# Attention with keys and queries kept once as high and low parts, logits and values in three passes

## The reference

```python
h = rmsnorm(x, norm_g)
xa, ga, q, ckv, gb, qi, ki, wi = split(h @ w_in)
# group A: causal convolution of 4 taps, two block-diagonal gates, real-gated linear recurrence
ya = rglru(xa) * silu(ga)
# group B: an indexer scores every causal key, each query keeps 256 keys of the shared latent c
c = rmsnorm(ckv)                                  # [1024, 256]
sel = top_k(sum_h relu(qi . ki) * wi, 256)
logits = (q @ w_uk) . c[sel] * 128**-0.5 + rel_bias[bucket(distance)]
o = softmax(logits) @ c[sel]                      # per head, [1024, 256]
yb = (o @ w_uv) * silu(gb)
x = x + concat(ya, yb) @ w_out
return rmsnorm(x, final_norm_g)
```

## Time and profile before

| | |
|---|---|
| median of the runs | 1614.35 us (1614.35, 1612.88, 1614.55) |
| the profiled execution | 1613.75 us; its span 1612.1 us, mean granted TensorE clock 0.995 |
| TensorE (PE), matmuls | 1580.3 us busy, 98% of the span, 7488 instructions |
| TensorE weight loads (PEld) | 1319.5 us, 82% |
| VectorE (DVE) | 847.6 us, 53% |
| GpSimd (POOL) | 645.1 us, 40% |
| ScalarE (ACT) | 581.5 us, 36% |
| chain that ended last | PE 90%, issue 4%, VectorE 2%, ScalarE 2%, GpSimd 1%, DMA 1% |

### The profile page before, as it was taken

One profiled execution on the slowest core, in us unless ns is written; L12 is line 12 of the kernel. 1 busy time (PEld: TensorE's weight loads), 2 busy tenths in 40 slices (PEclk: granted clock), 3 DMA queues, 4 the chain that ended last, 5 costly groups with the idle time before them and its releaser, 6 DMA issues.

```text
span 1612.1 us, 21577 instructions
## 1 busy us (share of the span) xinstructions
PE 1580.3 (98%) x7488; PEld 1319.5 (82%) x7488; DVE 847.6 (53%) x1483; ACT 581.5 (36%) x846; POOL 645.1 (40%) x477
## 2 busy tenths in 40 slices
PE   7999999999999999999999999999999899999998
PEld 6788999888888888888888888777776788888886
DVE  5347555577777877875555554377678000040003
ACT  6344555443444443332111111355555122222321
POOL 4334444434445444533444434212123244444650
PEclk9999999999999999999999999999999999999999
DMA  7212111122212122223222221322222522337322
GB/s 260 73 46 72 46 39 39 33 56 63 62 56 62 36 65 68 68 85 98 72 78 72 73 76 59 111 66 82 68 79 92 219 94 95 102 112 293 129 81 104
DMA packets 132345, 140.37 MB, mean 87 GB/s; under 512 B 8534, under 2 KB 103880, under 8 KB 130248
## 3 DMA queue, kind: packets, MB, share of 16 engines
q1 hardware_dynamic: 130760, 135.51, 26.4%
q0 software_dynamic: 1536, 4.20, 0.8%
HBM read 115.04 MB, written 24.64 MB: 87 GB/s over the span
## 4 chain that ended last, share of the span: by engine, by line
PE 90%; issue 4%; DVE 2%; ACT 2%; POOL 1%; DMA 1%; SPq 0%; DVEq 0%; ACTq 0%; POOLq 0%
PE ps L1099 17%; PE ps L1101 17%; PE ps L1100 17%; PE ps L1329 6%; PE ps L1330 6%; PE ps L1331 6%; PE ps L1294 4%; PE ps L1317 3%; PE ps L1203 2%; PE ps L1205 2%; PE ps L1281 2%; PE ps L1301 1%; PE ps L1421 1%; PE ps L1419 1%; PE ps L1420 1%
## 5 line engine op out<-in xcount | busy, mean ns | idle before, releaser
L1099 PE MATMUL ps<-hT_hi,w_lo 128*128 128x512 f32 (+1 forms) x1344 | 511.3, 380 | 0.0
L1100 PE MATMUL ps<-hT_lo,w_hi 128*128 128x512 f32 (+1 forms) x1344 | 509.2, 379 | 0.0
L1101 PE MATMUL ps<-hT_hi,w_hi 128*128 128x512 f32 (+1 forms) x1344 | 509.2, 379 | 0.0
L695 POOL TENSOR_TENSOR w_lo<-w_raw,w_hi 128x512 fp32r<-128x512 f32 x168 | 237.0, 1411 | 554.7 <-ACT w_hi L792 554.7
L1099 PEld LDWEIGHTS ps<-hT_hi,w_lo 128*128 128x128 f32 x1344 | 252.3, 188 | 44.7 <-issue 1.6
L1100 PEld LDWEIGHTS ps<-hT_lo,w_hi 128*128 128x128 f32 x1344 | 252.4, 188 | 43.4 <-issue 0.2
L1101 PEld LDWEIGHTS ps<-hT_hi,w_hi 128*128 128x128 f32 x1344 | 252.3, 188 | 42.5
L792 ACT ACTIVATE w_hi<-w_raw 128x512 fp32r<-128x512 f32 x168 | 105.9, 631 | 483.2 <-PE ps L1101 353.6
L693 POOL TENSOR_TENSOR w_raw<-w_raw,g_col 128x512 f32<-128x512 f32 x168 | 200.0, 1191 | 7.6 <-DMA w_raw<-in_w_in 7.6
L1329 PE MATMUL ps<-wo_hi,hT_lo 128*128 128x512 f32 x448 | 175.8, 392 | 4.2 <-POOL wo_lo L724 4.1
L1719 DVE TENSOR_TENSOR res<-ps,res 128x512 f32<-128x512 f32 x32 | 21.9, 691 | 294.9 <-PE ps L1331 244.8
(11 more groups left out here) (196 smaller groups left out, 1814.0 us busy)
## 6 DMA issues: line engine op xcount, KB each, us to landing
w_raw<-in_w_in SPq DMA_DIRECT2D x168, 256.0 KB, 2.8
wo_raw<-in_w_out SPq DMA_DIRECT2D x64, 512.0 KB, 3.6
xin<-in_x SPq DMA_DIRECT2D x8, 1024.0 KB, 6.9
res<-in_x SPq DMA_DIRECT2D x8, 1024.0 KB, 9.5
out<-res SPq DMA_DIRECT2D x16, 512.0 KB, 3.9
y_lru_dram<-sg SPq DMA_DIRECT2D x8, 512.0 KB, 2.8
q_dram<-av SPq DMA_DIRECT2D x8, 512.0 KB, 3.7
gate_dram<-rg SPq DMA_DIRECT2D x8, 512.0 KB, 4.2
```

Source lines behind the costliest of these rows:

```text
L695: nc.gpsimd.tensor_tensor(w_lo[:, j, :, :], part, w_hi[:, j, :, :].bitcast(F32), ALU.subtract).then_inc(w_lo_s, 1)
L1099: nc.tensor.matmul(o, wlo, hi, start=(kt == 0), stop=False)
L1100: nc.tensor.matmul(o, whi, lo, start=False, stop=False)
L1101: return nc.tensor.matmul(o, whi, hi, start=False, stop=(kt == KT - 1))
```

## The change

- **Logits** are three fp32r passes. Keys are kept as k_hi and k_lo (high_k on ScalarE, low_k on VectorE), queries as q_hi and q_lo, cut in the projection turns (ScalarE writes q_out_hi, VectorE q_out_lo in low_q) and stored as two tensors. There is one copy of k_hi, k_lo, q_hi, q_lo where kT and qT were double.
- **Values** are made for two heads at once (PAIRS = 4), in three fp32r passes of 256 columns, from hT_hi, hT_lo and wv_hi, wv_lo. In heads 0 to 5 the slots after blocks 0 and 1 each hold one quarter of the next pair's values. ScalarE copies each to vP, of which there are two.
- **Keys** of the next head move from the slot after block 0 into the slot after turn_p(h, 5), in two halves (keys_half), each into the half of X[1] where read_out(h, 0) and read_out(h, 1) stood.
- **Weights**: the parts of w_uk and w_uv are made once, beside attention projection turns 0 and 1, and stored to DRAM; wk_hi, wk_lo, wv_hi, wv_lo are loaded per head or pair. high_wk and low_wk go away.
- **Recurrent outputs**: high_y on ScalarE and low_y on GpSimd cut y in the recurrent stage, from the buffer sg, and both parts are stored. In the heads they are only loaded, into hT_hi and hT_lo.
- **Output stage**: EARLY has two groups in place of three; buffers lie elsewhere; the loads of w_out wait for other things.
- The loops over pairs of heads are written out for the eight heads.

The core of the diff (removed lines of pe_head and act_head are left out; the listing has them):

```diff
-EARLY = [(0, 0), (0, 1), (1, 0)]
+EARLY = [(0, 0), (0, 1)]
...
-        kT = [s3(f"kT{i}", [P, S]) for i in range(2)]
-        vN = [s3(f"vN{i}", [P, QB, HD]) for i in range(2)]
+        vP1 = s3("vP1", [P, QB, 2, HD])
+        k_hi = s3("k_hi", [P, S], F32R)
+        k_lo = s3("k_lo", [P, S], F32R)
+        vP0 = s3("vP0", [P, QB, 2, HD])
+        vP = [vP0, vP1]
...
-        qT = [qT0, qT1]
...
+        q_hi = s3("q_hi", [P, S], F32R)
+        q_lo = s3("q_lo", [P, S], F32R)
...
             with sp.Fori(1, G) as g:
                 lru_loads(g)
-                sp.wait_ge(y_lru, g + 1)
-                sp.dma_start(yl_d[ds(g - 1, 1)].rearrange("o p s -> (o p) s"), sg[:, :]).then_inc(y_st, 16)
                 gate_loads(g)
+                y_stores(g - 1)
...
+            def q_stores(h):
                 sp.wait_ge(pj_free[1], h + T_ATT // 2 + 2)
-                sp.dma_start(q_d[ds(h, 1)].rearrange("o p s -> (o p) s"), av[:, :]).then_inc(q_st, 16)
+                sp.dma_start(qh_d[ds(h, 1)].rearrange("o p s -> (o p) s"), q_out_hi[:, :].bitcast(F32)).then_inc(q_hi_st, 16)
+                sp.dma_start(ql_d[ds(h, 1)].rearrange("o p s -> (o p) s"), q_out_lo[:, :].bitcast(F32)).then_inc(q_lo_st, 16)
...
             att_loads(0)
-            sp.wait_ge(y_lru, G + 1)
-            sp.dma_start(yl_d[G - 1], sg[:, :]).then_inc(y_st, 16)
-
             sp.dma_start(wuk[:, :, :], a["w_uk"][0].rearrange("h d c -> d h c")).then_inc(wuk_in, 16)
+            y_stores(G - 1)
...
+            def head_loads(h):
+
+                sp.wait_ge(k_mm_s, 2 * h + 2)
+                wk_loads(h + 1)
+                sp.wait_ge(lg_mm, 8 * h + 4)
+                q_loads(h + 1, 0)
+                if h > 0:
+                    sp.wait_ge(lg_used, 8 * h)
+                tb_load(h + 1)
+                if h == 0:
+                    sp.wait_ge(v_mm_s, 4)
+                    wv_loads(1)
+                if h < G - CT:
+                    y_loads(h, y_ld)
+                if h in (1, 3):
+                    sp.wait_ge(v_mm_s, 2 * h + 6)
+                    wv_loads((h + 3) // 2)
+                sp.wait_ge(lg_mm, 8 * h + 8)
+                q_loads(h + 1, 1)
+
+            for h in range(NH - 1):
+                head_loads(h)
...
+            def low_y(g):
+
+                pool.wait_ge(y_hi_s, g + 1)
+                nc.gpsimd.tensor_tensor(y_lo[:, :], sg[:, :], y_hi[:, :].bitcast(F32), ALU.subtract).then_inc(y_lo_s, 1)
+
+            with pool.Fori(1, T_LRU + 2) as t:
+                low(t)
+            with pool.Fori(1, G) as g:
+                low(g * 2 + T_LRU)
+                low(g * 2 + (T_LRU + 1))
+                low_y(g - 1)
+            low(T_ATT)
+            low_y(G - 1)
...
+            def high_y(g):
+                act.wait_ge(y_lru, g + 2)
+                nc.scalar.activation(y_hi[:, :], sg[:, :], ACT.Copy).then_inc(y_hi_s, 1)
+
             def lru(g, first=False):
                 par = lambda k: lru_p[:, k, ds(g, 1)]
                 if not first:
-                    high(g * 2 + (T_LRU + 1))
+                    high(g * 2 + (T_LRU + 1), range(2))
+                    high_y(g - 1)
+                    high(g * 2 + (T_LRU + 1), range(2, PIECES))
...
+            def high_k(h, k):
+
+                act.wait_ge(k_mm_s, 2 * h + k + 1)
+                part = slice(k * NT, (k + 1) * NT)
+                nc.scalar.activation(k_hi[:, part], X[1][:, part], ACT.Copy).then_inc(k_hi_s, 1)
+
+            def copy_v(i, n, bank):
+
+                act.wait_ge(v_mm_s, 4 * i + n + 1)
+                nc.scalar.activation(vP[i % 2][:, 2 * n:2 * n + 2, :, :].rearrange("p t o d -> p (t o d)"), bank,
+                                     ACT.Copy).then_inc(v_cp, 1)
...
+            def act_head(h):
+                last = h == NH - 1
                 for q in range(QB):
                     p_copy(h, q)
                     if q + 1 == QB and not last:
                         softexp(h + 1, 0)
                         softexp(h + 1, 1)
...
+                    elif q + 2 < QB and q not in (2, 5):
                         softexp(h, q + 2)
...
+                    if q < 2 and h < NH - 2:
+                        copy_v(h // 2 + 1, 2 * (h % 2) + q, X[1][:, q * NT:(q + 1) * NT])
                     if q == 1:
+                        softexp(h, 4)
+                    if last and q == 3:
+                        act.wait_ge(ro_mm, 4 * (NH - 2) + 4)
+                        out_high(0, [0])
+                    if q == 5:
                         if not last:
...
+                            high_k(h + 1, 0)
+                        softexp(h, 7)
                         if not last:
...
+                            high_k(h + 1, 1)
+                        else:
+                            out_high(0, [1])
...
+            def keys_half(h, k):
+
+                pe.wait_ge(wk_ld, 32 * h + 32)
+                if h > 0:
+                    pe.wait_ge(o_used, 4 * h + 1 + k)
+                keys(X[1][:, k * NT:(k + 1) * NT], k).then_inc(k_mm_s, 1)
+
+            def values(i, n, bank):
+
+
+                pe.wait_ge(wv_ld, 32 * i + 32)
+                for s in range(2):
+                    tok = slice((2 * n + s) * P, (2 * n + s + 1) * P)
+                    o = bank[:, s * 2 * HD:(s + 1) * 2 * HD]
+                    for t in range(CT):
+                        hi, lo = (hT[:, G - CT + t, tok] for hT in (hT_hi, hT_lo))
+                        whi, wlo = (w[:, t, :, :].rearrange("p o d -> p (o d)") for w in (wv_hi, wv_lo))
+                        nc.tensor.matmul(o, lo, whi, start=(t == 0), stop=False)
+                        nc.tensor.matmul(o, hi, wlo, start=False, stop=False)
+                        last = nc.tensor.matmul(o, hi, whi, start=False, stop=(t == CT - 1))
+                last.then_inc(v_mm_s, 1)
+
+            def logits(h, q):
                 w = (q + 1) * P
-                if q == 0:
-                    pe.wait_ge(qb_ld[p], turn * 32 + 32)
-                    pe.wait_ge(kv_cp, 4 * h + 2)
+                if q % 4 == 0:
+                    pe.wait_ge(q_ld[q // 4], 32 * h + 32)
+                    pe.wait_ge(k_lo_s, 2 * h + q // 4 + 1)
                 pe.wait_ge(p_cp, 8 * h + q + 5 - LAST[q])
+                tok = slice(q * P, (q + 1) * P)
                 for n in range(0, w, NT):
                     e = min(n + NT, w)
-                    last = nc.tensor.matmul(LG[q][:, n:e], qT[p][:, q * P:(q + 1) * P], kT[p][:, n:e],
-                                            start=True, stop=True)
+                    nc.tensor.matmul(LG[q][:, n:e], q_lo[:, tok], k_hi[:, n:e], start=True, stop=False)
+                    nc.tensor.matmul(LG[q][:, n:e], q_hi[:, tok], k_lo[:, n:e], start=False, stop=False)
+                    last = nc.tensor.matmul(LG[q][:, n:e], q_hi[:, tok], k_hi[:, n:e], start=False, stop=True)
                 last.then_inc(lg_mm, 1)
...
                 pe.wait_ge(p_cp, 8 * h + 2 * pr + 6)
                 if pr == 0:
-                    pe.wait_ge(kv_cp, 4 * h + 4)
-                if pr < 2 and not last_head:
-                    pe.wait_ge(kv_cp, 4 * h + pr + 7)
+                    pe.wait_ge(v_cp, 4 * (h // 2) + 4)
+                if pr < 2 and h < NH - 2:
+                    pe.wait_ge(v_cp, 2 * h + pr + 5)
+                elif pr >= 2 and h < NH - 1:
+                    pe.wait_ge(k_lo_s, 2 * h + pr + 1)
                 else:
                     pe.wait_ge(o_used, 4 * h + pr + 3)
...
+            def pe_head(h):
+                last = h == NH - 1
                 for q in range(QB):
                     if q > 0:
                         turn_p(h, q)
                     if q in (3, 4, 6):
...
+                        read_out(h, {3: 0, 4: 1, 6: 2}[q])
                     if 0 < q < QB - AHEAD:
...
+                        logits(h, q + AHEAD)
+                    elif q > 5 and not last:
+                        logits(h + 1, 2 * q - 12)
+                        logits(h + 1, 2 * q - 11)
+                    if q < 2 and h < NH - 2:
+                        if h > 0:
+                            pe.wait_ge(o_used, 4 * h + q + 3)
+                        else:
+                            pe.wait_ge(v_cp, q + 3)
+                        values(h // 2 + 1, 2 * (h % 2) + q, X[1][:, q * NT:(q + 1) * NT])
+                    if q == 5 and not last:
+                        keys_half(h + 1, 0)
+                        keys_half(h + 1, 1)
+                    if last and q > 5:
+                        out_early(0, q - 6)
+                read_out(h, 3)
                 if not last:
                     turn_p(h + 1, 0)
...
+            keys_half(0, 0)
+            keys_half(0, 1)
+            for n in range(2):
+                values(0, n, X[0][:, n * NT:(n + 1) * NT])
             pe.wait_ge(pj_free[0], TILES // 2 + 2)
             pe.wait_ge(pj_free[1], TILES // 2 + 1)
...
+            for q in range(4):
+                logits(0, q)
+            for n in range(2):
```

(42 more changed lines are left out.)

443 lines of the change are left out of this document (210 added, 233 removed).

## The result

The changed kernel takes 1648.91 us (median of 4 runs, 1648.67 to 1650.6) against 1614.45 (4 runs, 1612.88 to 1614.94): a ratio of 1.0225, 95% interval 1.0213 to 1.0237. It is slower by 34 to 38 us where 22 were forecast. The profiled execution took 1648.99 us, its span 1647.2.

What follows compares the result with a forecast made beforehand. TensorE, busy 98%, bounded the kernel; after the change a head loop through VectorE's products and the keys would. Terms +18.2 + 2.6 + 2.5 + 2.3 - 1.0 - 2.5 = +22.1 on 1613.75 gave 1636 us, range 1620 to 1650.

Steps and rivals of the forecast that it cites:

- Keys inside the loop of the products: Heads: keys' halves wait for gated(h, 0) and gated(h, 1), TensorE waiting about 1.6 and 1.9 us; loop 29.2 us.
- The ping-pong: Heads: VectorE alternating with ScalarE, from gated(h, 3) to the end of gated(h+1, 0), takes 14.8 us.
- 29.2 instead of 26.6, 2.6 more in each of the 7 heads: Heads that make keys for a successor: serial steps lengthen the loop, +18.2 us in all, bounds +14 to +26.
- rival 2: Heads: the clock falls as well behind the two TensorE waits, 2.3 us more per head, 1652 us; chance 0.08.
- Recurrent boundary: Last recurrent turn: high_y and low_y delay the next tile's weights, TensorE waits; +2.6 us, bounds 1.3 to 3.6.
- the forecast of 0: Recurrent turns 0 to 6: high_y, low_y and the stores cost nothing because weights are far ahead; 0 us.
- Start of attention: Before and in head 0: late logits and value matmuls +2.5 us, late weights of pair 1 +2.3 us.
- The wait for the weights of pair 1: Head 0: weights load only when pair 0 is multiplied, TensorE waits 3.4 us; +2.3, bounds 1 to 4.
- Head 7: Last head: no keys there, shorter logits and no low_y on GpSimd; -1.0 us, bounds 0 to -2.
- Output: Output stage: wait for the fifth weight piece shrinks by about 1.7, clock may not fall; -2.5 us, bounds 0 to -4.
- each of eleven steps: Head loop's upper bound: 0.1 us more at each step makes 3.7 more a head, +26 us.
- Rival 1: Heads: TensorE's own work still decides and the ping-pong shrinks, -14 us, 1600 us; chance 0.13.

Runs made afterwards that it cites:

- e_fill: Changed kernel with eight unused matmuls of 512 columns on TensorE between the two halves of the keys; 1644.01 us.
- e_thin: Changed kernel with one pass instead of three in the logits of blocks 4 to 7, for timing only; 1649.73 us.
- e_swap: Changed kernel with the product gated(h, 1) ahead of the subtraction low_k(h + 1, 0) on VectorE; 1637.75 us.
- e_lowy: Changed kernel with the cut of the last recurrent output moved behind the next tile's weights on ScalarE and GpSimd; 1647.84 us.
- e_gates: Changed kernel with gated(h, 0) and gated(h, 1), each with its cut, one turn earlier in all heads but the last; 1622.30 us.
- e_best: Changed kernel with both boundaries mended and earlier products, key copies and block 2 copy; 1605.76 us, ratio 0.9954 to the kernel before.
- e_late_keys: Kernel before with only its keys moved to the slot of the change, ScalarE's copies moving along; 1625.74 us against 1612.12.

## Why the prediction was wrong in size, and right in mechanism

- **Keys inside the loop of the products: right.** Both waits, their releaser and their lengths came as forecast, and where the clock stays up the loop is 29.10 (e_fill, and 29.09 in e_thin). The ping-pong from one product to the end of the next, forecast 14.8, goes from 1142.44 to 1156.94 in the changed kernel, 14.50: ScalarE's removed copies and GpSimd's removed subtractions gave at most 0.3 there. What the forecast did not see is VectorE's own work between the two products, which takes as long as half 0 with ScalarE's copy: with the subtraction out of the way the loop is still 28.47 (e_swap).
- **The step that failed: a wait was priced at its length.** "29.2 instead of 26.6, 2.6 more in each of the 7 heads" left out that the clock falls behind it. I had this as rival 2 with a chance of 0.08 at 2.3 us a head, because the trace showed a single wait of 1.93 with no harm. It came in six of the seven heads, at 1.6, which covers the 8.9 us by which the heads exceed the forecast: from half 1 to read-out 2 it takes 3.61 us in head 3 (1160.54 to 1164.15) and 2.21 in head 0, where the clock held (1070.00, below, to the read-out at 1072.21); and read-out 2 takes 2.77 instead of 2.54.

```profile
1066.56 0.47 PE L1340 MATMUL ps<-hT_hi,wk_lo 128*128 128x512 f32 x1 [1.41 <-DVE yf L1770]
...
1070.00 0.47 PE L1340 MATMUL ps<-hT_hi,wk_lo 128*128 128x512 f32 x1 [1.83 <-DVE yf L1770]
...
1071.45 0.93 PE L1384 MATMUL ps<-ident,prob_sb 128*128 128x128 f32 x7
```

- **Recurrent boundary: wait right (2.57, forecast 2.6), term mis-sized**, 4.4, by the half clock behind it again. In the other turns the forecast of 0 held: without the wait the stretch is as long as before (e_lowy), and the convolution's taps on VectorE took 1.28 us beside low_y, as they did before.
- **Start of attention: mechanism right, sizes off.** The wait for the weights of pair 1 was 4.87, not 3.4: the second of the two loads landed 4.4 us after its issue, beside loads of queries and y, not 2.8; then the granted clock was 0.57 from 1048 to 1056 us. The term was +10.4 with the first loop, not +7.4. The logits started 6.69 us after the first key matmul, 6.29 before: +0.4 for +0.9.
- **Head 7: right (-1.1). Output: -0.7 for -2.5, by a cost that the forecast did not have.** The wait for the fifth piece of w_out went from 4.09 to 2.60 and no low clock follows it, as forecast, yet the 1440 matmuls from there to the end of the span took 337.8 us instead of 336.8. They are slower one by one, at full clock and without a wait: a hundred w_out matmuls take 22.92 us from start to start in the changed kernel and 22.67 before, which is 3.1 us over the 1248 of them. e_fill, e_gates and e_best, which share the new buffers, have 22.92 too; e_late_keys, which has the old ones, has 22.67. The w_in matmuls beside the attention projections have the same distance in both (0.228). What in the new layout does it was not tested.
- **The bounds.** Added up, the forecast's own bounds give 1627 to 1650, not 1625 to 1648. The result, 1648.91, lies at their upper end, and its lying there at all is luck: the upper bound stood for 0.1 us more at each of eleven steps, and what came was the half clock and the slower output.
- **Rival 1 (TensorE's work decides)** is refuted by e_thin for this order of the instructions, and comes true in e_best once the waits are gone. The advice on gaps that I set beside rival 2 (the Trainium skill, TensorE: Matmul & The Clock Gate, Why this matters for your kernels) pointed the right way, but it is meant for gaps longer than either of the two waits. Here the clock fell behind 1.57 and 1.84 us, and the measurement decides.

## What to carry to other kernels

Find the second chain before subtracting work from the busiest engine: when a product goes into a slot guarded by buffers that the other engines free late, the slot's waits become the loop, and moving the instruction that frees the buffer (4.0 us a head here, 1.6 of it the clock) can be worth more than the work saved. The boundary where ScalarE and GpSimd feed TensorE had too little slack here for 3.5 us of "side" work (1.06 and 2.42). And price a TensorE wait of 1.5 us or more at its length and at the half clock that may follow: 1.6 us a head behind the pair here, 1.8 behind the 2.57.
